# Bidirectional mLSTM recurrence: the decay moved onto the queries, carried and weighted products summed in one PSUM bank, and transposes and value maps cut into 64-row halves

## The chip, the cores and the metric

The kernel runs on one core of one Trainium2 chip. The metric is the device time in microseconds. Three runs of the kernel before gave 1169.3 to 1170.23 us, with a median of 1169.8 us. All data are float32; the big products are float32 values split into a high and a low part.

## The reference

Two blocks follow each other. The change lies in the first, in the recurrence of its mLSTM branch. For each of 4 heads of width 256, for 2 directions and for 8 chunks of 128 positions, it computes

```
b = cumsum(fj);  log_inter = b + m
m_t = max(log_inter, max(log_D))
inter_w = exp(log_inter - m_t)                        # one number per position
s = (q k^T) * exp(log_D - m_t)
num = s v + inter_w * (q C)                           # C is 256 x 256, carried
den = sum(s) + inter_w * (q n)                        # n is carried
h = num / max(|den|, exp(-m_t))
C, n = decay * C + (ws * k)^T v,  decay * n + sum(ws * k)
```

The queries and values are block-diagonal maps, with blocks of 4, of a convolved input and of the input. Both directions are summed, normalised per head, scaled, gated and multiplied by the output weights.

## The kernel before, in words

**Before and after the recurrence.** Input projections by split products (lines 918 to 920, three products for one) run until 487 us, with features on the partitions. The recurrence runs from there to 676 us. Then come the output product of the first block, its normalisation, and the second block.

**The unit.** The recurrence is written out by hand as 64 units: head h, pair p of a head (0 to 7), direction d, so n = 16 h + 2 p + d (`unit`). For a unit, TensorE does in `units` (line 1179): the carried product, queries times state, two matmuls of 257 columns (line 1194), not in the first pair of a head; filler work for the next head; the weighted product, `Pm` times values, one matmul of 257 columns (line 1210); and the state update, weighted keys `kwb` times values, two matmuls (line 1219), not in the last pair. Column 257 is a column of ones, which carries the denominator. The carried product has bank 0 for itself, the weighted one banks 4 to 7 in turn, the update banks 2 and 3, and all filler work bank 1 (`free` is cut to one bank by `del free[1:]`). `take` makes TensorE wait until the last user of a bank has been read out.

**Filler work.** While head h runs, `headwise(h + 1, i)` makes the features of the next head, one i in each of the units 0 to 11 (`FILL`): i from 0 to 3 the queries (line 1135, 512 columns), 4 to 7 the keys turned over (line 1145, four transposes of 128 x 128), 8 to 11 the values (line 1147, four products of 128 x 128 with `bdh`, a 128 x 128 block-diagonal weight). `scores` in units 12 and 14 makes queries times keys (line 1158). `turn_h` turns the normalised output of the head before over (line 1172) at the end of units 7, 9, 11 and 13 (`TURN`). For head 0 the features and scores are made in one piece ahead of the first unit; for head 3 there is no next head, and a few groups of the output product take the filler's place (`AHEAD`).

**ScalarE**, per unit (line 2402): `weight(n + 1)` makes the exponentials `Wb` (line 2368); `spread` issues the DMA that spreads the rows of -m over all partitions four pairs ahead (line 2359); then the carried product is copied out of bank 0, multiplied by `cols[:, 0, r]`, the decay of each position, into `tmpi` or `tmpj` (line 2415); then the filler's banks are copied out (lines 2340 to 2351), outputs of the head before are normalised, split or turned (lines 2399, 2393, 2376).

**GpSimd**, per unit: `Pm` = scores times `Wb` (line 783), `kwb` = keys times a weight per position (line 749), in even units the mask added (line 755), and for the head before the gate and the low half (lines 762 and 770).

**VectorE**, per pair (line 1821): `total` adds `tmp` to the weighted product in its bank (line 1794), `state` updates the state (line 1773, or 1776 in the first pair), then the denominators (lines 1835 to 1837), `output` (lines 1805, 1808), and statistics and skip part (lines 1719, 1725, 1757).

```
                ps = filled(ve, "t_intra", n + 1, "v_h", n + 1)
                if p:
                    ve.wait_ge(s["a_tmp"], upd_of(h, p - 1, d) + 1)
                    ve.tensor_tensor(ps[:, 0:AUG], ps[:, 0:AUG], tmps[p % 2][:, d, :], ALU.add
                                     ).then_inc(s["v_tot"], 1)
```

Here `filled` waits for TensorE's product; the second wait is for ScalarE's scaled copy.

Of the kernel before, what the change touches and what calls it, by code (L numbers as in the profile page):

```python
# [13 lines left out]
P = 128  # L14
# [92 lines left out]
def build(nc, I, out):  # L107
# [64 lines left out]
    nm_t = nc.dram_tensor("nmax", [ROWS, P], F32)  # L172
# [4 lines left out]
    with ctx:  # L177
# [12 lines left out]
        def sem(name):  # L190
# [7 lines left out]
        (u_hi, u_lo, qT0, qT1, kt0, kt1, v0, v1, ST0, ST1, Wb, yt1, tmpj, smzb, h2, Q, y2a, _q, y2b, glu, _h, agb, _b, pTd, pTb) = region(  # L198
# [6 lines left out]
             ("yt1", [P, HALF], F32), ("tmpj", [P, 2, AUG], F32),  # L205
# [23 lines left out]
        def y2(j, part):  # L229

            if j < 4:
# [7 lines left out]
         hc0, yt0, kwb, Amat, hc1, Cst, tmpi, Pm, bdh, gs, nM, cols,  # L239
# [19 lines left out]
             ("tmpi", [P, 2, AUG], F32), ("Pm", [P, 2, P], F32), ("bdh", [P, 2, P], F32),  # L259
# [13 lines left out]
        hcs, tmps = (hc0, hc1), (tmpi, tmpj)  # L273
        gsum = cva[:, 0, :]
        yts = (yt0, yt1)

        def brd(q):
            place = hc1 if q < 4 else wraw
            return place[:, q % 4, :].rearrange("p (d t) -> p d t", d=2)

        def rows_of(q):
            r0, r1 = unit(2 * q)[4], unit(2 * q + 1)[4]
            return bass.AP(nm_t, r0 * P, [[0, P], [(r1 - r0) * P, 2], [1, P]])
# [25 lines left out]
        bank = [ctx.enter_context(nc.psum_tensor(f"bank{i}", [P, 512], F32)) for i in range(4)]  # L309
        wide = [ctx.enter_context(nc.psum_tensor(f"wide{m}", [P, S], F32)) for m in range(2)]  # L310
        bank += [wide[i // 2][:, i % 2 * 512:(i % 2 + 1) * 512] for i in range(4)]
# [14 lines left out]
            "v_tot v_h v_hn v_y1 v_h2 v_lnv v_nmr v_xh v_x2lo v_bnv v_ln2 v_ug v_sp v_yab v_cv2 v_s v_rc "  # L326
            "v_o v_cg v_pT v_y2lo v_r2 v_gain v_out "

            "v_rel a_w0 a_ss a_sd a_uhi a_px a_mixhi a_sz a_yhi a_um a_c a_mz a_gsum a_r a_hq a_st a_W a_tmp a_t1 "
# [20 lines left out]
        FILL = {m: (m,) for m in range(12)}  # L350
# [96 lines left out]
        def _(sp_):  # L447
# [101 lines left out]
            for n in range(16):  # L549
# [19 lines left out]
                if n == 13:  # L569
                    sp_.wait_ge(s["v_r"], 3)  # L570
                    sp_.dma_start(nm_t.ap(), nM[:, :]).then_inc(s["o_rel"], 16)
                    sp_.wait_ge(s["o_rel"], 32)
                    for q in range(4):
                        sp_.dma_start(brd(q), rows_of(q)).then_inc(s[f"l_br{q}"], 16)
# [28 lines left out]
            sp_.wait_ge(s["a_W"], NU)  # L603
            wt(W_OM + 2)
# [74 lines left out]
        def _(g_):  # L679
# [53 lines left out]
            def heads_blocks(h):  # L733

                if h:
                    g_.wait_ge(s["t_hw"], 12 * h)
                else:
                    g_.wait_ge(s["t_gsum"], 2)
# [34 lines left out]
            def units(h):  # L773
                g_.wait_ge(s["a_hq"], 12 * h + 8)
# [117 lines left out]
        def _(pe):  # L892
# [225 lines left out]
            turns, free = [0], [1, 5, 2, 6, 3, 7]  # L1118
# [7 lines left out]
            def headwise(h, i):  # L1126


                n, i = i // 4, i % 4
                if n == 0:  # L1130
# [3 lines left out]
                    ps = fill("a_hq", 12 * h + i + 1)  # L1134
                    mm = pe.matmul(ps[:, :], Amat[:, 2 * h + m, :], cc[:, 2 * h + m, nh * HALF:(nh + 1) * HALF],  # L1135
                                   start=True, stop=True)
                else:
                    ps = fill("a_hq", 12 * h + 4 * n + i + 1)
                    if n == 2 and i == 0:
                        pe.wait_ge(s["g_bdh"], 2 * h + 2)  # L1140
                    for b in range(4):
                        t, m = 2 * i + b // 2, b % 2
                        tt = slice(t * P, (t + 1) * P)
                        if n == 1:
                            mm = pe.transpose(ps[:, b * P:(b + 1) * P], cc[:, 2 * h + m, tt], idn)
                        else:
                            mm = pe.matmul(ps[:, b * P:(b + 1) * P], um[:, 2 * h + m, tt], bdh[:, m, :],  # L1147
                                           start=True, stop=True)
# [1523 lines left out]
```

## Time and profile before

| what | before |
|---|---|
| median of 3 runs (lowest, highest) | 1169.8 us (1169.3, 1170.23) |
| span of the profiled execution | 1168.5 us |
| TensorE matmul busy | 1158.7 us, 99% |
| VectorE busy | 678.5 us, 58% |
| ScalarE busy | 359.2 us, 31% |
| GpSimd busy | 455.9 us, 39% |
| instructions | 17252 |

The span is the time from the first to the last instruction in one profiled execution; no time of its own is given for that execution beside the span, and the median of the runs is 1.3 us above it. Busy shares are averages over stages: TensorE's 99% says that it bounds most of the program, and not what an engine costs inside the recurrence. A matmul's recorded duration includes its way through the array, so the cost of one in a dense row is the distance of the starts, not the mean duration.

### The profile page before, as it was taken

How to read it: one execution, taken by the hardware profiler on the slowest of the kernel's cores; microseconds unless marked ns; L12 is line 12 of the kernel's file. 1: busy time of each engine (PE TensorE's matmuls, PEld its weight loads, DVE VectorE, ACT ScalarE, POOL GpSimd, SP SyncE). 2: the span in 40 equal slices, each digit the busy share in tenths (PEclk: the TensorE clock that was granted, in tenths of full speed). 3: DMA queues.
4: the chain of work that ended last, by engine and by line, in shares of the span. 5: the costliest groups of instructions: out<-in, count | busy, mean ns of one | idle time of the engine just before them, and what ended most of it. 6: DMA issues, size and time to landing. Idle time of an engine off the chain costs nothing.

```text
span 1168.5 us, 17252 instructions
## 1 busy us (share of the span) xinstructions
PE 1158.7 (99%) x6599; PEld 946.1 (81%) x6599; DVE 678.5 (58%) x1249; ACT 359.2 (31%) x720; POOL 455.9 (39%) x437
## 2 busy tenths in 40 slices
PE   9999999999999999999999999999999999999997
PEld 6888888888888868888878888878988887777786
DVE  5645557334368502157777883894699434556668
ACT  6312121100012212445665631242111134553322
POOL 2424222223333223354657656304223323455534
PEclk9999999999999999999999999999999999999999
DMA  7321121343312112300113242123121130133113
GB/s 241 109 81 45 36 81 36 123 152 114 109 36 72 64 64 90 101 23 23 50 34 112 88 171 73 72 100 95 40 88 36 37 100 1 38 122 124 39 38 141
DMA packets 75075, 93.56 MB, mean 80 GB/s; under 512 B 13938, under 2 KB 54090, under 8 KB 74483
## 3 DMA queue, kind: packets, MB, share of 16 engines
q1 hardware_dynamic: 67270, 88.73, 22.7%
q10 hardware_dynamic: 7724, 3.74, 1.2%
q8 instruction: 53, 0.87, 0.3%
q14 instruction: 28, 0.22, 0.1%
HBM read 75.11 MB, written 18.92 MB: 80 GB/s over the span
## 4 chain that ended last, share of the span: by engine, by line
PE 93%; DVE 4%; DMA 1%; ACT 1%; issue 1%; POOL 0%; ACTq 0%; DVEq 0%; POOLq 0%
PE bank L918 22%; PE bank L920 22%; PE bank L919 22%; PE bank L1219 4%; PE bank L1194 4%; PE wide L1210 2%; PE wide L1412 2%; PE bank L1158 1%; PE bank L1147 1%; PE bank L1135 1%; PE wide L920 1%; PE wide L919 1%; PE wide L918 1%; PE bank L1387 1%; DVE h L1910 1%; PE wide L1387 1%
## 5 line engine op out<-in xcount | busy, mean ns | idle before, releaser
L687 POOL CAST whi<-wraw 128x2048 fp32r<-128x2048 f32 x31 | 58.8, 1898 | 454.1 <-PE bank L920 404.1
L918 PE MATMUL bank<-u_hi,wlo 128*128 128x512 f32 x488 | 190.4, 390 | 0.0
L920 PE MATMUL bank<-u_hi,whi 128*128 128x512 f32 x488 | 189.9, 389 | 0.0
L919 PE MATMUL bank<-u_lo,whi 128*128 128x512 f32 x488 | 189.9, 389 | 0.0
L689 POOL TENSOR_TENSOR wlo<-wraw,whi 128x2048 fp32r<-128x2048 f32 x32 | 153.1, 4784 | 3.0 <-ACT whi L2488 0.5
L918 PE MATMUL bank<-x_hi,wlo 128*128 128x512 f32 x312 | 123.5, 396 | 0.0
L920 PE MATMUL bank<-x_hi,whi 128*128 128x512 f32 x312 | 121.6, 390 | 0.0
L919 PE MATMUL bank<-x_lo,whi 128*128 128x512 f32 x312 | 121.5, 389 | 0.0
L918 PEld LDWEIGHTS bank<-u_hi,wlo 128*128 128x128 f32 x488 | 91.6, 188 | 19.9 <-POOL wlo L689 0.8
L920 PEld LDWEIGHTS bank<-u_hi,whi 128*128 128x128 f32 x488 | 91.6, 188 | 19.0
L919 PEld LDWEIGHTS bank<-u_lo,whi 128*128 128x128 f32 x488 | 91.6, 188 | 18.9
L918 PEld LDWEIGHTS bank<-x_hi,wlo 128*128 128x128 f32 x312 | 58.5, 188 | 16.1 <-issue 4.3
L1990 DVE SCALAR_TENSOR_TENSOR wide<-glu,VT,wide 128x1024 f32<-128x1024 f32 x58 | 69.3, 1281 | 0.0
L920 PEld LDWEIGHTS bank<-x_hi,whi 128*128 128x128 f32 x312 | 58.5, 188 | 12.4
L919 PEld LDWEIGHTS bank<-x_lo,whi 128*128 128x128 f32 x312 | 58.6, 188 | 11.7
L862 POOL TENSOR_SCALAR sp<-sp,rcx 128x384 f32<-128x384 f32 (+1 forms) x64 | 37.9, 606 | 76.4 <-DVE rcx L2077 76.4
L1219 PE MATMUL bank<-v,kwb 128*128 128x257 f32 x224 | 58.3, 383 | 0.5 <-DVE Cst L1773 0.3
L1650 DVE SCALAR_TENSOR_TENSOR cva<-um,VT,cva 128x1022 f32<-128x1022 f32 (+1 forms) x32 | 58.0, 1812 | 1.1
L1194 PE MATMUL bank<-Cst,qT 128*128 128x257 f32 x224 | 58.0, 381 | 0.1
L2296 ACT ACTIVATE um<-bank 128x512 f32<-128x512 f32 x16 | 9.6, 599 | 155.7 <-PE bank L920 155.7
L783 POOL TENSOR_TENSOR Pm<-ST,Wb 128x128 f32<-128x128 f32 x64 | 29.1, 455 | 66.0 <-ACT Wb L2368 61.2
L918 PE MATMUL bank<-whi,ym_lo 128*128 128x512 f32 x128 | 51.2, 400 | 0.0
(391 smaller groups left out, 2440.9 us busy)
## 6 DMA issues: line engine op xcount, KB each, us to landing
wraw<-in_w_in SPq DMA_DIRECT2D x26, 1024.0 KB, 5.5
wraw<-in_w_out SPq DMA_DIRECT2D x12, 1024.0 KB, 5.1
xr<-in_x SPq DMA_DIRECT2D x8, 512.0 KB, 7.3
hst<-in_x SPq DMA_DIRECT2D x4, 1024.0 KB, 5.0
hpool<-hst SPq DMA_DIRECT2D x4, 1024.0 KB, 4.1
smz<-mzs SPq DMA_DIRECT2D x16, 256.0 KB, 2.0
h<-hpool SPq DMA_DIRECT2D x4, 1024.0 KB, 7.5
resid<-h SPq DMA_DIRECT2D x8, 512.0 KB, 2.6
```

The costliest lines, as they stand in the source:

```text
L687: g_.tensor_copy(whi[w % 2][:, :, :], wraw[:, :, :]).then_inc(s["w_hi"], 1)
L689: g_.tensor_tensor(wlo[w % 2][:, :, :], wraw[:, :, :], whi[w % 2][:, :, :].bitcast(F32), ALU.subtract).then_inc(s["w_lo"], 1)
L783: g_.tensor_tensor(Pm[:, n % 2, :], STs[h % 2][:, ck, :], Wb[:, n % 2, :], ALU.mult).then_inc(s["g_P"], 1)
L862: g_.tensor_scalar(row, row, rcx[:, x % 2, i:i + 1], 0.5 if g else 1.0, ALU.mult, ALU.mult).then_inc(s["g_nm"], 1)
L918: pe.matmul(ps, al, bh, start=(k == 0), stop=False)
L919: pe.matmul(ps, ah, bl, start=False, stop=False)
L920: return pe.matmul(ps, ah, bh, start=False, stop=(k == nk - 1))
L1194: mm = pe.matmul(ps[:, 0:AUG], q[:, k, ck * P:(ck + 1) * P], Cst[:, d, k, :], start=(k == 0), stop=(k == 1))
L1210: pe.matmul(ps[:, 0:AUG], Pm[:, n % 2, :], v[:, ck, :], start=True, stop=True).then_inc(s["t_intra"], 1)
L1219: mm = pe.matmul(ps[:, 0:AUG], kwb[:, m % 2, k * P:(k + 1) * P], v[:, ck, :], start=True, stop=True)
L1650: ins = ve.scalar_tensor_tensor(acc[:, a0:a1], um[:, j, a0 + sh:a1 + sh], tap(q), acc[:, a0:a1], ALU.mult, ALU.add)
L1990: ins = ve.scalar_tensor_tensor(dst, src, w, acc, ALU.mult, ALU.add)
```

## The change

1. **Decay.** The rows exp(log_inter - m_t), in `r4[:, 0, :]`, are written to DRAM beside the rows of -m, and spread over all partitions with them (256 columns for 128). VectorE multiplies the queries of a chunk by them (`scale_q`, line 1826 of the new code), one pair ahead, into `qsi` or `qsj`. The multiplication by `cols[:, 0, r]` in ScalarE's copy goes, and with it the copy itself.
2. **One bank.** The carried product, of the scaled queries, is written into the bank of the weighted product (`start=(k == 0), stop=False`), and the weighted product is added there by TensorE (`start=(p == 0)`). VectorE's `total` goes. The bank is taken ahead of the carried product.
3. **Halves.** Keys turned over, value maps and, for heads 0 to 2, the output turned over are cut into products of 64 rows and 64 columns: rows 0 to 63 into one bank, rows 64 to 127 into the next. An i now covers 8 blocks of 128 x 128, not 4, and `FILL` puts them into units 4, 6 (keys) and 8, 10 (values). The filler has banks 0 and 1.

The core of the diff:

```diff
-            turns, free = [0], [1, 5, 2, 6, 3, 7]
+            turns, free = [0], [5, 6, 7, 4]
...
+            def both(m, name, value):
+
+                take(2 * m, name, value)
+                return take(2 * m + 1, name, value)
...
+                both(m2, "a_hq", 10 * h + (i + 1 if i < 6 else 2 * i - 4))
+                if i == 6:
+                    pe.wait_ge(s["g_bdh"], 2 * h + 2)
+                for block in range(8):
+                    t, m = i % 2 * 4 + block // 2, block % 2
+                    tt = slice(t * P, (t + 1) * P)
+                    for half in range(2):
+                        rows = slice(64 * half, 64 * half + 64)
+                        out_ = bank[2 * m2 + half][:, block * 64:(block + 1) * 64]
+                        if i < 6:
+                            mm = pe.transpose(out_, cc[rows, 2 * h + m, tt],
+                                              cst[rows, C_ID + 64 * half:C_ID + 64 * half + 64])
                         else:
-                            mm = pe.matmul(ps[:, b * P:(b + 1) * P], um[:, 2 * h + m, tt], bdh[:, m, :],
-                                           start=True, stop=True)
+                            mm = pe.matmul(out_, um[rows, 2 * h + m, tt], bdh[rows, m, rows], start=True, stop=True)
...
-        FILL = {m: (m,) for m in range(12)}
+        FILL = {0: 0, 1: 1, 2: 2, 3: 3, 4: 4, 6: 5, 8: 6, 10: 7}
...
+                    both(0, "a_t1", n + 1)
+                    for b in range(4):
+                        for half in range(2):
+                            rows = slice(64 * half, 64 * half + 64)
+                            mm = pe.transpose(bank[half][:, b * 64:(b + 1) * 64],
+                                              hcs[h % 2][rows, 4 * nh + b, mt * P:(mt + 1) * P],
+                                              cst[rows, C_ID + 64 * half:C_ID + 64 * half + 64])
...
+                    sums = take(4 + n % 4, "v_h", n + 1)
                     if p:
                         i = upd_of(h, p - 1, d)
+                        pe.wait_ge(s["v_qs"], i + 1)
                         pe.wait_ge(s["v_C"], 2 * i + 2)
-                        ps = take(0, "a_tmp", i + 1)
                         for k in range(2):
-                            mm = pe.matmul(ps[:, 0:AUG], q[:, k, ck * P:(ck + 1) * P], Cst[:, d, k, :],
-                                           start=(k == 0), stop=(k == 1))
+                            mm = pe.matmul(sums[:, 0:AUG], scaled_q(i)[:, k, :], Cst[:, d, k, :],
+                                           start=(k == 0), stop=False)
...
-                    ps = take(4 + n % 4, "v_h", n + 1)
-                    pe.matmul(ps[:, 0:AUG], Pm[:, n % 2, :], v[:, ck, :], start=True, stop=True
+                    pe.matmul(sums[:, 0:AUG], Pm[:, n % 2, :], v[:, ck, :], start=(p == 0), stop=True
...
+                    ve.tensor_tensor(scaled_q(i), qTs[h % 2][:, :, ck * P:(ck + 1) * P],
+                                     carried(n // 2, d).unsqueeze(1).to_broadcast([P, 2, P]), ALU.mult
+                                     ).then_inc(s["v_qs"], 1)
...
-                    total(h, n)
+                    if p < NT - 1:
+                        scale_q(h, p + 1)
                     if p or h in (0, NH - 1):
                         state(h, n)
-                    total(h, n + 1)
-                    if p:
-                        ve.wait_ge(s["v_tot"], upd_of(h, p - 1, 1) + 1)
+                    ve.wait_ge(s["t_intra"], n + 2)
...
+                    sp_.wait_ge(s["a_r"], 3)
+                    sp_.dma_start(nm_t.ap()[:, 1, :], r4[:, 0, :]).then_inc(s["o_rel"], 16)
```

**How instructions move, 1.** TensorE, ahead of the first unit, the features of head 0. Before, from the last two query maps to the scores:

```order
L1135 MATMUL bank<-cc,Amat 128x512
L1145 MATMUL wide<-cst,cc 128x128 x4
L1145 MATMUL bank<-cst,cc 128x128 x4
L1145 MATMUL wide<-cst,cc 128x128 x4
L1145 MATMUL bank<-cst,cc 128x128 x4
L1147 MATMUL wide<-bdh,um 128x128 x4
L1147 MATMUL bank<-bdh,um 128x128 x4
L1147 MATMUL wide<-bdh,um 128x128 x4
L1147 MATMUL bank<-bdh,um 128x128 x4
L1158 MATMUL wide<-qT,cc 128x128 x8
```

And now:

```order
L1152 MATMUL wide<-cc,Amat 128x512 x4
L1165 MATMUL bank<-cst,cc 128x64 x32
L1168 MATMUL wide<-bdh,um 128x64 x32
L1178 MATMUL bank<-qT,cc 128x128 x16
L1152 MATMUL bank<-cc,Amat 128x512
```

Sixteen transposes and sixteen value products of 128 columns have become 32 and 32 of 64 columns, in one row behind each other.

**How instructions move, 2.** TensorE, units 4 and 5 of head 0 (`wide` is the pair of banks of the weighted product). Before:

```order
L1194 MATMUL bank<-Cst,qT 128x257 x2
L1145 MATMUL bank<-cst,cc 128x128 x4
L1210 MATMUL wide<-v,Pm 128x257
L1219 MATMUL bank<-v,kwb 128x257 x2
L1194 MATMUL bank<-Cst,qT 128x257 x2
L1145 MATMUL bank<-cst,cc 128x128 x4
L1210 MATMUL wide<-v,Pm 128x257
```

And now:

```order
L1222 MATMUL wide<-Cst,qsj 128x257 x2
L1165 MATMUL bank<-cst,cc 128x64 x16
L1237 MATMUL wide<-v,Pm 128x257
L1246 MATMUL bank<-v,kwb 128x257 x2
L1222 MATMUL wide<-Cst,qsj 128x257 x2
L1237 MATMUL wide<-v,Pm 128x257
```

The 257-column products are as many as before; both units' transposes now stand in one group of 16 halves in unit 4, and unit 5 has no filler.

**How instructions move, 3.** VectorE, one middle pair of head 0. Before:

```order
L1794 TENSOR_TENSOR wide<-wide,tmpj 128x257
L1773 SCALAR_TENSOR_TENSOR Cst<-Cst,cols,bank 128x257 x2
L1794 TENSOR_TENSOR wide<-wide,tmpj 128x257
L1835 TENSOR_TENSOR den<-wide,cols 128x2
L1836 SCALAR_TENSOR_TENSOR den<-wide,den 128x2
L1837 RECIPROCAL den<-den 128x2
```

And now:

```order
L1826 TENSOR_TENSOR qsj<-qT,wraw 128x256 x2
L1800 SCALAR_TENSOR_TENSOR Cst<-Cst,cols,bank 128x257 x2
L1867 TENSOR_TENSOR den<-wide,cols 128x2
L1868 SCALAR_TENSOR_TENSOR den<-wide,den 128x2
L1869 RECIPROCAL den<-den 128x2
```

Two additions in PSUM, one ahead of and one behind the first state update, have become two multiplications with both inputs in SBUF, both ahead of it.

## Rows read from the trace of the kernel before

**Rows 1.** The page: busy time of each engine, share of the span, instructions.

```profile
PE 1158.7 (99%) x6599; PEld 946.1 (81%) x6599; DVE 678.5 (58%) x1249; ACT 359.2 (31%) x720; POOL 455.9 (39%) x437
```

**Rows 2.** Busy by stretch: heads 0, 1, 2, and two pairs late in head 3.

```profile
core 0: us, PE busy (x) PEld busy (x) DVE busy (x) ACT busy (x) POOL busy (x), PEclk, DMA share, GB/s
499.00:542.60 43.60, 43.60 (x234) 37.59 (x234) 27.89 (x82) 19.92 (x45) 19.51 (x41) 1.00 0.09 23
542.60:589.40 46.80, 46.58 (x250) 38.58 (x249) 34.62 (x105) 29.89 (x63) 28.10 (x46) 1.00 0.14 40
589.40:636.30 46.90, 46.68 (x250) 38.36 (x248) 34.82 (x105) 30.30 (x64) 30.49 (x49) 1.00 0.17 46
660.80:671.50 10.70, 10.70 (x53) 8.79 (x52) 9.79 (x27) 6.02 (x14) 10.70 (x15) 1.00 0.18 52
```

**Rows 3.** Timeline of PE: start, time to the last end, what. Head 0's features.

```profile
490.03 0.60 PE L1145 MATMUL wide<-cst,cc 128*128 128x128 f32 x4
...
491.77 1.06 PE L1147 MATMUL wide<-bdh,um 128*128 128x128 f32 x8
...
495.35 1.95 PE L1158 MATMUL wide<-qT,cc 128*128 128x128 f32 x16
```

**Rows 4.** Timeline of PE: transposes in 64-row halves elsewhere, and their neighbours.

```profile
786.23 0.71 PE L1251 MATMUL wide<-cst,h 64*128 64x64 f32 x16
786.87 0.50 PE L1301 MATMUL bank<-x_hi,whi 128*128 128x512 f32 x1
...
937.38 0.39 PE L920 MATMUL bank<-x_hi,whi 128*128 128x512 f32 x1
937.70 1.21 PE L1251 MATMUL wide<-cst,Q 64*128 64x64 f32 x32
938.84 0.50 PE L918 MATMUL bank<-x_hi,wlo 128*128 128x512 f32 x1
939.17 0.39 PE L919 MATMUL bank<-x_lo,whi 128*128 128x512 f32 x1
```

**Rows 5.** Timeline of PE: products (not transposes) on two alternating tiles.

```profile
1063.85 0.88 PE L1412 MATMUL wide<-pT,vt 128*64 128x128 f32 x12
1064.55 0.83 PE L1412 MATMUL wide<-pTc,vt 128*64 128x128 f32 x12
```

**Rows 6.** Timeline of ACT ahead of the first unit: table load, last values, first scores.

```profile
492.80 1.28 ACT L2368 ACT_TABLE_LOAD   x1
...
495.84 0.61 ACT L2345 ACTIVATE v<-bank 128x512 f32<-128x512 f32 x1
497.33 0.60 ACT L2351 ACTIVATE ST<-wide 128x512 f32<-128x512 f32 x1 [0.89 <-PE wide L1158]
```

**Rows 7.** Timeline of PE in head 1: a late unit.

```profile
551.99 1.03 PE L1219 MATMUL bank<-v,kwb 128*128 128x257 f32 x4
553.07 1.11 PE L1194 MATMUL bank<-Cst,qT 128*128 128x257 f32 x4
554.02 0.60 PE L1145 MATMUL bank<-cst,cc 128*128 128x128 f32 x4
```

**Rows 8.** Timeline of ACT and DVE at the same place: the copy and its addition.

```profile
552.47 0.46 ACT L2415 ACTIVATE tmpj<-bank,cols 128x257 f32<-128x257 f32 x1
553.03 0.43 DVE L1794 TENSOR_TENSOR wide<-wide,tmpj 128x257 f32<-128x257 f32 x1 [1.43 <-ACT tmpj L2415]
```

**Rows 9.** Groups of instructions: sum, mean ns, idle before. SBUF-only and PSUM operations of DVE.

```profile
L1794 DVE TENSOR_TENSOR wide<-wide,tmpj 128x257 f32<-128x257 f32 x32 | 13.8, 431 | 18.4 <-PE wide L1210 11.1 <-ACT tmpj L2415 7.1
L1738 DVE TENSOR_SCALAR hc<-hc,mv,rs 128x256 f32<-128x256 f32 x8 | 2.7, 407 | 0.0
```

**Rows 10.** Timelines of DVE and POOL in head 3, at a DVE pass over SBUF alone.

```profile
665.28 0.95 DVE L1757 SCALAR_TENSOR_TENSOR yt<-cc,VT,yt 128x512 f32<-128x512 f32 x1
665.66 0.92 POOL L749 TENSOR_SCALAR kwb<-kt,cols 128x256 f32<-128x256 f32 x1
...
668.22 0.47 POOL L749 TENSOR_SCALAR kwb<-kt,cols 128x256 f32<-128x256 f32 x1
```

More of the change, by code:

```diff
@@ L238, in build @@
          cva, mzs, _m, wgx, gx, gr, ga, wkx, kx, ak,
-         hc0, yt0, kwb, Amat, hc1, Cst, tmpi, Pm, bdh, gs, nM, cols,
+         hc0, yt0, kwb, Amat, hc1, Cst, qsi, Pm, bdh, gs, nM, cols,
          rif, rl, rb, r4, rz, rp, rpc, rms8, rn,
@@ L307, in build @@
         rcx = sb("rcx", [P, 2, 2])
-        bank = [ctx.enter_context(nc.psum_tensor(f"bank{i}", [P, 512], F32)) for i in range(4)]
+        duo = [ctx.enter_context(nc.psum_tensor(f"bank{m}", [P, S], F32)) for m in range(2)]
         wide = [ctx.enter_context(nc.psum_tensor(f"wide{m}", [P, S], F32)) for m in range(2)]
-        bank += [wide[i // 2][:, i % 2 * 512:(i % 2 + 1) * 512] for i in range(4)]
+        duo += wide
+        bank = [duo[i // 2][:, i % 2 * 512:(i % 2 + 1) * 512] for i in range(8)]
         names = (
@@ L1133, in headwise @@
                         pe.wait_ge(s["g_am"], KT)
-                    ps = fill("a_hq", 12 * h + i + 1)
-                    mm = pe.matmul(ps[:, :], Amat[:, 2 * h + m, :], cc[:, 2 * h + m, nh * HALF:(nh + 1) * HALF],
-                                   start=True, stop=True)
[L1137 to L1145, printed above, removed]
-                        else:
-                            mm = pe.matmul(ps[:, b * P:(b + 1) * P], um[:, 2 * h + m, tt], bdh[:, m, :],
-                                           start=True, stop=True)
+                    ps = fill("a_hq", 10 * h + i + 1)
+                    pe.matmul(ps[:, :], Amat[:, 2 * h + m, :], cc[:, 2 * h + m, nh * HALF:(nh + 1) * HALF],
+                              start=True, stop=True).then_inc(s["t_hw"], 1)
+                    return
+                both(m2, "a_hq", 10 * h + (i + 1 if i < 6 else 2 * i - 4))
[10 more added lines that the diff above has]
+                                              cst[rows, C_ID + 64 * half:C_ID + 64 * half + 64])
+                        else:
+                            mm = pe.matmul(out_, um[rows, 2 * h + m, tt], bdh[rows, m, rows], start=True, stop=True)
                 mm.then_inc(s["t_hw"], 1)
             def scores(h, b):
-                pe.wait_ge(s["a_hq"], 12 * h + 4)
+                pe.wait_ge(s["a_hq"], 10 * h + 4)
                 ps = fill("a_st", 2 * h + b + 1)
@@ L1223, in units @@
                         turn_h(h - 1, TURN[n % 16])
-            for i in range(12):
-                headwise(0, i)
+            for i in range(8):
+                headwise(0, i, i % 4)
+            free[:] = [0, 1]
             for b in range(2):
                 scores(0, b)
-            del free[1:]
             for h in range(NH):
@@ L2341, in evac_features @@
                                   ).then_inc(s["a_hq"], 1)
-                elif i < 8:
-                    ac.activation(kts[h % 2][:, t:t + 2, :], pv, ACT.Copy).then_inc(s["a_hq"], 1)
-                else:
-                    ac.activation(vs[h % 2][:, t:t + 2, 0:HD], pv, ACT.Copy).then_inc(s["a_hq"], 1)
+                    return
+                ac.wait_ge(s["t_hw"], 8 * h + i + 1)
+                t = slice(i % 2 * 4, i % 2 * 4 + 4)
+                if i < 6:
+                    ac.activation(kts[h % 2][:, t, :].rearrange("p t (m u c) -> p u (t m) c", m=2, c=64),
+                                  duo[m2][:, :].rearrange("p (u b c) -> p u b c", u=2, c=64), ACT.Copy
+                                  ).then_inc(s["a_hq"], 1)
+                    return
+                for half in range(2):
+                    ac.activation(vs[h % 2][:, t, 0:HD].rearrange("p t (m u c) -> p u t m c", m=2, c=64)[:, half],
+                                  bank[2 * m2 + half][:, :].rearrange("p (t m c) -> p t m c", t=4, c=64), ACT.Copy
+                                  ).then_inc(s["a_hq"], 1)
             def evac_scores(h, b):
@@ L2409, in units @@
                         spread(n // 2 + 4)
[L2410 to L2416 removed]
                     if h + 1 < NH:
[L2418 to L2419 removed]
+                        if m in FILL:
+                            evac_features(h + 1, FILL[m])
                         if m in (12, 14):
```

110 lines of the change are left out of this document (56 added, 54 removed).

## The prediction

> **What bounds the kernel now.** I read the page first, then the busy time by stretch, then single places on the timelines. On the page TensorE is busy 99% of the span and VectorE, the next, 58% [rows 1]. The change touches only the recurrence, from 490 to 676 us, so that is where to look. The busy times by stretch [rows 2] show TensorE busy in 43.60 of 43.60 us while head 0 runs; so what head 0's stretch costs is what TensorE is given. Heads 1 and 2 take 46.80 and 46.90 us. They have four turns of an output more, each of 4 x 0.109 = 0.44 us (the transposes of rows 3: four in 0.43), which makes 43.6 + 1.7 = 45.3; the other 1.5 us per head are waits. Late in head 3, where TensorE has no features to make, GpSimd is busy for all of 10.70 us and VectorE for 9.79: there TensorE is no longer alone at the bound, and a pair takes 5.35 us. TensorE was granted its full clock (1.00, the 2.4 GHz level) in each stretch, so no term is about the clock. The span is 1168.5 us; the runs' median lies 1.3 us above it, outside the recurrence, so I take differences of the span off the median.
>
> **What costs TensorE nothing and gives it nothing.** The decay part leaves TensorE with the same two products of 257 columns per unit, only in another bank. It takes 56 copies from ScalarE and swaps 56 additions on VectorE for 56 multiplications. By itself it can pay only through waits. What pays directly is the halves.
>
> **Step 1, the price of a half.** The trace has transposes in halves elsewhere [rows 4]: 16 of them start at 786.23 and the next matmul at 786.87, 0.64 us; 32 take from 937.70 to 938.84, 1.14 us. So 16 more cost 0.50: 31 ns for one, 62 ns for the two halves of a block, against 0.43 / 4 = 109 ns for a whole transpose [rows 3]; and 0.14 us are fixed. Going in costs more: from 937.38 to 937.70 are 0.32 us, where such a matmul takes 0.23; and the one behind takes 0.33 (938.84 to 939.17), 0.10 too much. That is 0.33 us around each group of halves; behind it here stands a matmul of another kind, whose slow start is 0.08 (553.07 to 554.02 is 0.95, where four take 0.87 [rows 7]). I take 0.31.
>
> A page of the Trainium skill speaks of this: "TensorEngine Tiling (Array Packing)", sections "Theoretical Speedup" and "Key Properties". It gives up to 2 times for 64 rows, and says that changing the tiling mode drains the engine. The rows agree with the drain and put 0.31 us on it; the speed-up they show is 1.75 and not 2. By a full 2 times without the drain all steps on halves together would give about 13 us.
>
> **Step 2, head 0's features.** Keys and values now take from 490.03 to 495.35, 5.32 us [rows 3]. Afterwards there are 16 pairs of key halves and 16 pairs of value halves. A value product is float32 and no transpose, so it goes through twice (eight records for four blocks, 0.89 us). Whether the two halves' passes run side by side, as transposes do, no row shows for this tile form. The nearest are 12 passes of 128 columns on two alternating tiles in 0.70 us, 58 ns each, where whole ones take 111 [rows 5, 3]; so yes. 16 + 32 = 48 slots of 62.5 ns are 3.0, with one change in and out 3.3 us: 2.0 gained. ScalarE takes part of it: its work here is a table load and copies, and its last value copy ends at 496.45 [rows 6]. The amount that it copies stays (the keys' copies are twice as long and half as many), so the first score copy, which began at 497.33, can begin at about 496.6 and end at 497.2. TensorE is back in the first unit at 497.05 and needs that bank at once, so 0.2 to 0.3 us of waiting come. **-1.7 us**, bounds 0 (ScalarE and GpSimd hold it) and -2.0. The second DRAM write ahead of the spread (SyncE's queue, and the stores of the gate's rows behind it) delays the first mask by about 3 us; it is not needed until the first `Wb`, behind the table load at 492.80, so it is covered.
>
> **Step 3, the features of heads 1 to 3.** Keys: 16 x 0.109 = 1.74 us become 2 x (0.50 + 0.31) = 1.62, 0.12 gained. Values: 4 x 0.89 = 3.57 become 2 x (1.00 + 0.31) = 2.62, 0.95 gained. Three heads of 1.07: **-3.2 us**. Bounds: 0.25 us around a group gives -3.9, 0.40 gives -2.1.
>
> **Step 4, the turned outputs.** Four blocks in halves cost 0.25 + 0.31 = 0.56 us against 0.44: a loss of 0.12 each, since the group is too short for its changes. Eight in heads 1 and 2: **+1.0 us**. Four more in head 3 lie beside work that is the bound there.
>
> **Step 5, waits that go.** In heads 1 and 2 ScalarE is late after its table loads. Its copy out of bank 0 runs from 552.47 to 552.93, and TensorE starts the next carried product at 553.07 instead of 552.86, then needs 0.08 to come up to speed [rows 7, 8]. The addition on VectorE is late by the same copy (idle 1.43 us, ended by it [rows 8]), and the update behind it waits too. That is 2 x 0.29 us per head, on waits that no longer exist: **-1.15 us**, bounds 0 and -1.5 (the waits between a turn and the next filler, on ScalarE's other copies, stay). Next in line are `Wb`, `Pm` and `kwb`, which come earlier as ScalarE has 56 x 0.47 us less.
>
> **Step 6, the scaled queries.** One addition on VectorE takes 0.43 us with PSUM, a pass of 256 columns in SBUF 0.41 [rows 9]: the same. They are made a pair ahead, so TensorE waits for the state and not for them. But they read two inputs in SBUF. Late in head 3 the one such pass of VectorE (665.28) goes along with a `kwb` of 0.92 us on GpSimd, which takes 0.47 when it is alone, and takes 0.95 itself [rows 10]. So the two engines shut each other out, and now two passes per pair do so. The additions, with an input in PSUM, did not. In head 3 GpSimd has no idle time [rows 2]: two passes of 0.35 to 0.4 us more in each of two to three pairs are +1.4 to +2.4 us; VectorE's idle time for ScalarE, some 0.5 us per pair, goes. **+1.5 us**, bounds -0.5 and +2.5. In heads 0 to 2 GpSimd is busy 20 to 30 of 44 to 47 us and hides it.
>
> The page "SBUF — State Buffer" of the Trainium skill, section "SBUF: two separate sides", has this as a rule: a VectorE operation with two SBUF inputs and a GpSimd operation that reads SBUF lock each other out for the whole instruction. The trace agrees, 0.92 against 0.47 us.
>
> **Sum.** -1.7 - 3.2 + 1.0 - 1.15 + 1.5 = -3.6. From 1169.8 this gives **1166.2 us**; what lies behind the recurrence moves with it, since the output product and all behind it wait for TensorE.
>
> **Rivals.**
> - *The lock costs in heads 1 and 2 as well.* From unit 9 on GpSimd has the gate of the head before, and a pair of it is 5.35 us in all heads; two locks make it 6.1, against TensorE's 5.7 to 7. A late `Pm` or `kwb` costs at least 0.29 us [rows 7]. Once in each of the last four pairs of two heads: +2.3, so 1168.5, no difference that counts. For it: GpSimd's full row in head 3. Against it: 16 to 19 us of idle time per head [rows 2].
> - *Nothing is gained ahead of unit 0 and at the waits* (ScalarE decides both): 1169.0.
> - *The passes of the value halves don't overlap*, so that it ends slower. The two passes of one half use the same rows of the array; if the other half's issue waits behind the second, a slot holds one pass and not two. A group of 8 blocks is then 32 x 0.0625 + 0.31 = 2.3 us instead of 1.31, and 1.79 before. Eight groups: +8 on the forecast, 1174.2. It decides from about 0.19 us per block on, where the sum is zero. Against it: rows 5.
>
> **How the numbers follow.** A measurement of this kernel tells 0.2%, 2.3 us, from no change. Forecast, with steps between their bounds: 0.70, nearly all of it below 1167.5. Lock everywhere or nothing gained at the start: 0.20. Slower: 0.10, most of it the passes, some of it waits on the new order that I don't see. The lower end is the good bound of each step together with a head 3 that loses nothing (-2.0 - 3.5 + 1.0 - 1.3 - 0.3 = -6.1, 1163.7); the upper end takes in the second rival, 1169.2.
>
> **What would show it.** Right: 4 blocks of value halves in some 0.5 us and a group behind a switch of 0.3; features of head 0 in 3.3 us; heads 0 to 2 at about 42.5, 45.2 and 45.2 us; no wait on ScalarE's copy of the carried product; head 3 longer by about 1.5 us with `kwb` or the scaling often at twice its time. Wrong: value halves at 0.25 us per block; waits of TensorE on `Pm`, `kwb` or the scaled queries in heads 0 to 2; or a head 3 that is shorter.

## The result and the profile after

The changed kernel takes 1172.97 us (median of 8 runs, 1172.6 to 1174.44) against 1169.54 for the kernel before (8 runs beside it, 1169.3 to 1170.23): ratio 1.0029, 95% interval 1.0019 to 1.0039. It is 3.4 us slower, where 3.6 us less were forecast. The profiled execution took 1172.75 us with a span of 1170.9 us, in front of 1168.5 before.

The busy row of its page answers to [rows 1]: TensorE 240 instructions more, ScalarE 64 copies fewer.

```profile
PE 1159.4 (99%) x6839; PEld 942.0 (80%) x6839; DVE 685.2 (59%) x1249; ACT 333.6 (28%) x656; POOL 463.6 (40%) x437
```

The stretches of [rows 2] were not cut at the same events in each head; head 2 ended 2.1 us too early there. I cut both traces anew, from the first weighted product (`Pm`) of a head to that of the next, and in head 3 to that of its last unit. In the changed kernel all cuts lie at the second pass of that product, 0.22 us behind the first, which leaves the lengths as they are. Busy time by stretch, the kernel before:

```profile
499.80:543.36 43.56, 43.56 (x234) 37.55 (x233) 28.06 (x83) 19.66 (x45) 19.48 (x40) 1.00 0.10 24
543.36:590.21 46.85, 46.63 (x250) 38.63 (x249) 34.94 (x107) 29.94 (x62) 28.15 (x47) 1.00 0.14 40
590.21:638.45 48.24, 48.02 (x257) 39.77 (x256) 35.92 (x110) 30.43 (x63) 31.83 (x50) 1.00 0.19 51
638.45:676.73 38.28, 37.89 (x178) 31.35 (x177) 33.45 (x101) 21.76 (x46) 27.10 (x42) 1.00 0.36 119
```

and the same of the changed kernel:

```profile
498.91:543.09 44.18, 44.18 (x282) 36.99 (x281) 27.26 (x85) 12.40 (x29) 19.68 (x40) 1.00 0.15 48
543.09:590.85 47.76, 47.02 (x314) 37.56 (x313) 35.75 (x106) 23.54 (x46) 30.88 (x47) 1.00 0.20 62
590.85:639.86 49.01, 48.54 (x321) 38.77 (x320) 37.55 (x111) 24.06 (x47) 34.22 (x50) 1.00 0.23 71
639.86:679.80 39.94, 38.24 (x194) 30.93 (x193) 36.22 (x99) 18.50 (x37) 29.43 (x43) 1.00 0.37 128
```

So the heads take 0.62, 0.91, 0.77 and 1.66 us more, 3.96 in all; the stretch from head 0's first query map to its first weighted product takes 0.41 less (12.77 against 13.18, from the starts in the trace). Together +3.55, close to the 3.4 of the medians. Head 0 has no idle time of TensorE, so it has more to do; in heads 1, 2 and 3 TensorE's idle time grows, from 0.22, 0.22 and 0.39 us to 0.74, 0.47 and 1.70.

The spans differ by 2.4 us and not by 3.55, because two other parts are shorter in the changed kernel's trace. The part ahead of the first query map takes 0.7 us less, and over all traces of kernels with the change it varies by 0.6. The part behind the recurrence takes 0.47 less, and in all twelve traces of the changed kernel and its variants it takes 0.4 to 0.55 less than in the one trace before. Most of it is one wait that only the trace before has: there the weights of a later product (`wraw`) arrive late, VectorE waits 0.42 us for ScalarE's copy of them, and TensorE starts 0.4 us late behind VectorE (timeline of PE, before):

```profile
785.21 1.09 PE L1273 MATMUL wide<-cst,h 128*128 128x128 f32 x8 [0.24 <-DVE h L1910]
```

So the sums below, which count head 0's features and the heads alone, are up to 0.5 us higher than what the medians show.

**Halves.** Timeline of PE in head 0's features, which answers to [rows 3], and at a group of values in head 0's units:

```profile
489.44 1.21 PE L1165 MATMUL bank<-cst,cc 64*128 64x64 f32 x32
490.49 3.73 PE L1168 MATMUL wide<-bdh,um 64*128 64x64 f32 x64
494.15 3.84 PE L1178 MATMUL bank<-qT,cc 128*128 128x128 f32 x32
...
518.55 1.03 PE L1222 MATMUL wide<-Cst,qsj 128*128 128x257 f32 x4
519.51 2.00 PE L1168 MATMUL bank<-bdh,um 64*128 64x64 f32 x32
521.45 0.70 PE L1237 MATMUL wide<-v,Pm 128*128 128x257 f32 x2
521.98 0.60 PE L1246 MATMUL bank<-v,kwb 128*128 128x257 f32 x2
```

The 16 keys take 1.05 us (489.44 to 490.49), 66 ns a block, where 62 were forecast and a whole one takes 109. The 16 values take 3.66 us (to 494.15), 229 ns a block, and whole ones took 0.89 / 4 = 223 [rows 3]. Halves give nothing there: 0.09 of the 3.66 us is the change back to whole tiles, and the rest is 223 ns a block again. In the group at 519.51 eight blocks take 1.94 us, and the switch is paid on both sides: 0.96 from 518.55 where such a product takes 0.87, and 0.53 behind where 0.43 is usual.

**Waits.** Timeline of PE at head 1's first carried products, then of DVE at the same place:

```profile
545.02 0.60 PE L1237 MATMUL wide<-v,Pm 128*128 128x257 f32 x2
545.45 1.03 PE L1246 MATMUL bank<-v,kwb 128*128 128x257 f32 x4
547.23 1.11 PE L1222 MATMUL wide<-Cst,qsj 128*128 128x257 f32 x4 [0.74 <-issue]
```

```profile
544.78 0.76 DVE L1803 COPY Cst<-bank 128x257 f32<-128x257 f32 x2 [1.11 <-PE bank L1246]
545.46 0.39 DVE L1752 BATCH_NORM_AGGREGATE mv<-bn 128x2 f32<-128x6 f32 x2
545.76 0.72 DVE L1746 BATCH_NORM_STATS2 bn<-hc 128x6 f32<-128x256 f32 x2
546.40 1.07 DVE L1826 TENSOR_TENSOR qsj<-qT,wraw 128x256 f32<-128x256 f32 x2
```

The state has been there since about 545.5, but the product that uses it also needs the scaled queries. VectorE makes these (L1826) behind the state's copy and the statistics of head 0's last outputs; the first of the two passes ends at 547.13, and TensorE starts at 547.23. "issue" on PE's row is that wait: 1.78 us from the product before, where 0.87 is usual, 0.91 lost. In head 2, ahead of the product at 594.76, 0.6 us are lost in the same way. The lock has a share in both: the first pass takes 0.73 us in head 1 and 0.85 in head 2, beside GpSimd's work, where one takes 0.41 alone.

The third place is head 3. Timelines of DVE and of POOL there:

```profile
652.63 1.44 DVE L1826 TENSOR_TENSOR qsj<-qT,wraw 128x256 f32<-128x256 f32 x2
653.99 0.86 DVE L1800 SCALAR_TENSOR_TENSOR Cst<-Cst,cols,bank 128x257 f32<-128x257 f32 x2
```

```profile
652.89 0.89 POOL L768 TENSOR_TENSOR wraw<-wraw,msk 128x256 f32<-128x256 f32 x1
653.80 0.58 POOL L796 TENSOR_TENSOR Pm<-ST,Wb 128x128 f32<-128x128 f32 x1
```

Two scaling passes need 1.44 us beside GpSimd's work, where two take 0.83 otherwise; the state's update stands behind them, and TensorE behind that. Waits of PE in the recurrence:

```profile
PE bank L1246 <- DVE Cst L1800: 1.7, 3, 1.0
PE wide L1222 <- issue: 1.2, 2, 0.7
```

(us in total, times, longest). The copy of [rows 7, 8] is gone, and no wait on it is left.

### The profile page after: what moved, and what is told of

Same layout as the page of the kernel before. It is cut to its first block, busy times and chain, and to the rows that moved or that the text cites. A ratio compares the mean times of both kernels' runs of the same rounds, so it can differ in the third digit from the quotient of the medians.

```text
span 1170.9 us, 17563 instructions
## 1 busy us (share of the span) xinstructions
PE 1159.4 (99%) x6839; PEld 942.0 (80%) x6839; DVE 685.2 (59%) x1249; ACT 333.6 (28%) x656; POOL 463.6 (40%) x437
## 4 chain that ended last, share of the span: by engine, by line
PE 97%; DVE 2%; DMA 0%; issue 0%; ACT 0%; ACTq 0%; DVEq 0%
PE bank L931 24%; PE bank L933 23%; PE bank L932 23%; PE wide L1222 4%; PE bank L1246 4%; PE wide L1237 2%; PE wide L1439 2%; PE bank L1178 1%; PE bank L1168 1%; PE wide L931 1%; PE wide L933 1%; PE wide L932 1%; PE bank L1152 1%; PE bank L1414 1%; PE wide L1414 1%; PE bank L1426 1%
## 5 line engine op out<-in xcount | busy, mean ns | idle before, releaser
L796 POOL TENSOR_TENSOR Pm<-ST,Wb 128x128 f32<-128x128 f32 x64 | 33.7, 526 | 66.4 <-ACT Wb L2408 60.2
L1800 DVE SCALAR_TENSOR_TENSOR Cst<-Cst,cols,bank 128x257 f32<-128x257 f32 x96 | 41.8, 477 | 21.2 <-PE bank L1246 21.0
```

Of the source, the lines that this page charges most:

```text
L796: g_.tensor_tensor(Pm[:, n % 2, :], STs[h % 2][:, ck, :], Wb[:, n % 2, :], ALU.mult).then_inc(s["g_P"], 1)
L1800: ins = ve.scalar_tensor_tensor(Cst[:, d, k, :], Cst[:, d, k, :], cols[:, 4, r:r + 1], pu[:, 0:AUG], ALU.mult, ALU.add)
```

## The experiments

Theory: the value halves don't pay (their passes don't shorten), and the scaled queries sit in VectorE's order where TensorE has to wait for them, at the start of a head and, stretched by GpSimd, in head 3. Rival: what costs is the order of evacuation and the halves' copies, or the turned outputs. What no run varies is the new grouping of the filler work, 8 blocks at a time over two banks: every run below has it. "Head times" below are those from weighted product to weighted product as above. A ratio is against the kernel before on the same chip.

**One part undone or alone.** e1: the value maps as whole blocks (the copies out of the bank likewise).

```
-  mm = pe.matmul(out_, um[rows, 2 * h + m, tt], bdh[rows, m, rows], start=True, stop=True)
+  if half == 0:
+      whole = bank[2 * m2 + block // 4][:, block % 4 * P:(block % 4 + 1) * P]
+      mm = pe.matmul(whole, um[:, 2 * h + m, tt], bdh[:, m, :], start=True, stop=True)
```

> The changed kernel, with only its value maps made of whole 128 x 128 products again (still 8 blocks per filler, two banks). Theory A (a pass of a value product costs 0.11 us however few columns it has, so that halves only add the switch): the six groups in heads 0 to 2 lose 0.35 us each and head 0's features 0.1, so 2.2 us faster than the changed kernel, about 1170.8 us; a group of 8 blocks back at 1.79 us. Theory B (the loss comes from the scaled queries and waits): within 0.5 us of the changed kernel, 1173.

Measured: 1171.34 us (1170.64 to 1171.71), 1.0011 [1.0002, 1.0020]. Heads 0 to 2 take 43.49, 47.12 and 48.48 us, 0.69, 0.64 and 0.53 less than with halves; head 3 and the part ahead of head 0 are unchanged. The 16 value blocks ahead of unit 0 cost the same whole or in halves (12.77 us from the first query map either way), where they share one switch with the keys. Two groups a head cost 0.31 each on average, which is the price of one switch from the prediction.

e2: the turned outputs whole again.

```
-  for half in range(2):
-      rows = slice(64 * half, 64 * half + 64)
-      mm = pe.transpose(bank[half][:, b * 64:(b + 1) * 64],
-                        hcs[h % 2][rows, 4 * nh + b, mt * P:(mt + 1) * P],
-                        cst[rows, C_ID + 64 * half:C_ID + 64 * half + 64])
+  mm = pe.transpose(bank[0][:, b * P:(b + 1) * P],
+                    hcs[h % 2][:, 4 * nh + b, mt * P:(mt + 1) * P], idn)
```

> The changed kernel, with only the turned outputs of heads 0 to 2 whole again. Theory A: the eight turns in heads 1 and 2 cost 0.58 us in halves and 0.44 whole, so 1.2 us faster, about 1171.8; the four in head 3 lie beside VectorE's and GpSimd's bound and give 0 to 0.6 more. Theory B: no change, 1173.

Measured: 1172.85 us, 1.0023 [1.0014, 1.0032]. Heads: 44.18, 47.62, 49.16, 39.84; 0.09 us less in all, where 1.2 were expected. Behind a turn TensorE waits for the scores' bank: from the end of the update ahead of the turn to the scores are 1.53 us with a whole turn (577.69 to 579.22 in head 1) and 1.49 with halves, so there the halves' cost lies in a wait. In head 2 something else hides it: with whole turns the wait for the scaled queries at its start is 1.04 us and not 0.59. Without that growth the halves of heads 1 and 2 would cost 0.4 us, an estimate from these rows.

e3: the keys whole again.

```
-  mm = pe.transpose(out_, cc[rows, 2 * h + m, tt],
-                    cst[rows, C_ID + 64 * half:C_ID + 64 * half + 64])
+  if half == 0:
+      whole = bank[2 * m2 + block // 4][:, block % 4 * P:(block % 4 + 1) * P]
+      mm = pe.transpose(whole, cc[:, 2 * h + m, tt], idn)
```

> The changed kernel, with only the keys' transposes whole again. Theory A: head 0's features lose 0.7 us, the six groups in the heads change by under 0.04 each: 1173.6, slower than the changed kernel by 0.6. Theory B: no change.

Measured: 1174.0 us, 1.0035 [1.0021, 1.0048]. The part ahead of head 0 takes 0.75 us more (13.52), the heads 0.07, 0.07, 0.08 and 0.24 more. Keys in halves gain 1.2 us by this, of which the 0.24 in head 3, where no keys are made, have no cause that I can show.

e4: the decay part alone; keys, values and turns are all whole (e1, e2 and e3 together).

> The changed kernel with values, keys and turns all whole: what is left of the change is the decay on the queries and the shared bank. Theory A: 2.2 + 1.2 - 0.7 = 2.7 us faster than the changed kernel, 1170.3, so about 0.7 us slower than the kernel before, with the waits on the scaled queries at the start of heads 1 and 2 and in head 3 still there. Theory B (the decay is the whole loss): 1173, with the waits making 3.4 us against the kernel before.

Measured: 1171.92 us (1171.41 to 1173.47), 1.0016 [1.0007, 1.0024]. Heads: 43.56, 47.35, 48.70, 39.83, which is 0, +0.50, +0.46 and +1.55 on the kernel before. So 2.5 us of the 3.55 are the decay part (with the new grouping of the filler, which this run keeps), and the halves the other 1.0, where I had expected 2.7 for the halves.

**The order of the scaled queries.** e5, on e1: the queries of a head's first carried pair are scaled in the last pair of the head before, ahead of the statistics.

```
-  if p < NT - 1:
+  if p and p < NT - 1 or n == 0:
       scale_q(h, p + 1)
+  if p == NT - 1 and h < NH - 1:
+      scale_q(h + 1, 1)
```

> e1 (values whole), with the queries of a head's first carried pair scaled one pair earlier, ahead of the statistics of the head before. Theory C (TensorE waits at the start of heads 1 and 2 for scaled queries that stand on VectorE behind the statistics): the waits of 0.98 and 0.68 us go, 1.6 us faster than e1, about 1169.7. Theory D (VectorE is simply behind by its doubled passes, and the wait moves to the next thing it makes): under 0.5 us.

Measured: 1169.1 us (1168.77 to 1171.64), 0.9998 [0.9989, 1.0006]. Heads 1 and 2 fall from 47.12 and 48.48 to 46.12 and 47.53; head 3 keeps its 39.96. The wait at head 1's start is gone (timeline of PE of e5):

```profile
544.59 0.60 PE L1239 MATMUL wide<-v,Pm 128*128 128x257 f32 x2
545.02 1.03 PE L1248 MATMUL bank<-v,kwb 128*128 128x257 f32 x4
545.89 1.03 PE L1224 MATMUL wide<-Cst,qsj 128*128 128x257 f32 x4
```

e7, on e5: the state's update ahead of the scaling in each pair.

```
+  if p or h in (0, NH - 1):
+      state(h, n)
   if p and p < NT - 1 or n == 0:
       scale_q(h, p + 1)
   if p == NT - 1 and h < NH - 1:
       scale_q(h + 1, 1)
-  if p or h in (0, NH - 1):
-      state(h, n)
```

> e5 with, in every pair, the first state update ahead of the scaling. Theory O: TensorE's waits of 1.2, 0.58 and 0.65 us in head 3, for the state's banks, fall by what the two passes take there (1.4 us each), 1.5 us or more faster than e5, about 1168. Theory L (the lock's cost is throughput of VectorE and GpSimd and only moves): under 0.4 us faster than e5.

Measured: 1169.15 us, 0.9993 [0.9984, 1.0002]. Head 3 gains 0.40 (39.56), head 2 loses 0.54 (48.07). The order moves the wait and gains nothing in sum. It also brings the passes beside other work of GpSimd: 31 of the 56 take over 0.5 us, where 16 did in e5, and in head 2 TensorE waits 0.34 us for a late `Pm` (591.10).

**The lock.** e6, on e1: the scaling reads one tensor, with a column as a scalar; the decay at each position is left out, so that only one factor per partition is applied.

```
-  ve.tensor_tensor(scaled_q(i), qTs[h % 2][:, :, ck * P:(ck + 1) * P],
-                   carried(n // 2, d).unsqueeze(1).to_broadcast([P, 2, P]), ALU.mult
+  ve.tensor_scalar(scaled_q(i), qTs[h % 2][:, :, ck * P:(ck + 1) * P],
+                   cols[:, 0, r:r + 1], 1.0, ALU.mult, ALU.mult
```

> e1 with the scaling as a pass with one SBUF input and a number per partition, of the same size and at the same place; the decay of each position is left out, so the numbers are not the recurrence's. Theory L (the passes and GpSimd shut each other out because the passes read two SBUF inputs): two passes take 0.75 us and not 1.07 to 1.45, kwb stays at 0.48, and the waits fall by at least half: 1.5 to 2 us faster than e1, 1169.5. Theory O (the order is the cause: two passes stand ahead of the state update and behind the statistics, locked or not): the waits shrink only by the passes' own shortening, 0.6 us or less in all, 1170.8.

Measured: 1169.64 us (1169.55 to 1170.42), 1.0000 [0.9991, 1.0009]. Head 3 takes 39.02, 0.95 less than in e1, but the test isn't clean: the passes are shorter when alone, and still stretched. One line's instructions of e6 (ns: least/median/most):

```profile
L1828 DVE TENSOR_SCALAR qsi<-qT,cols x28: 331/355/2610, 490.5 to 665.6; 128x256 f32<-128x256 f32 x28
L1828 DVE TENSOR_SCALAR qsj<-qT,cols x28: 334/541/1351, 503.8 to 671.0; 128x256 f32<-128x256 f32 x28
```

The longest there (579.87, 1.35 us) begins under GpSimd's gate (L775) and ends 0.15 us behind it, so it waits for that too. So I needed a pass of equal length whose second input is in PSUM. Data for it are there only once the denominators have been read, so the pair e9 and e10 has the scaling there. e9, on e5: the two `if` blocks of e5 stand behind the denominators.

> e5 with the two scaling passes of each pair behind the denominators and ahead of the outputs, so that they no longer stand ahead of the first state update. Theory L (a lock costs VectorE and GpSimd time that no order gives back): head 3 up to its last weighted product stays within 0.5 us of e5's 39.96, the run within 0.5 us of 1169.1. Theory O (order): head 3 at 38.5 or less, 1167.7.

Measured: 1180.01 us (1179.85 to 1180.17), 1.0087 [1.0074, 1.0101], over 10 us above either expectation: both had looked at head 3, and heads 0 to 2 take 4.2, 2.9 and 3.3 us more than in e5. e10, on e9: the second input is the bank with the sums, and the operation a comparison instead of a product; the decay of the carried product is left out.

```
-  carried(n // 2, d).unsqueeze(1).to_broadcast([P, 2, P]), ALU.mult
+  wide[(at_q[0]) % 2][:, 0:2 * P].rearrange("p (k c) -> p k c", k=2), ALU.is_ge
```

> e9 with the second input of each scaling pass taken from the weighted product's PSUM bank and not from the spread rows in SBUF, and a comparison in place of the product; the decay is left out, so the numbers are not the recurrence's. Same size, same place, same number of passes. Theory L: no pass over 0.5 us, kwb back at 0.48 us but for the pass of the skip part, head 3 shorter than e9's by 1 to 1.7 us and the run at about 1168. Theory O: the same times as e9 within 0.4 us.

Measured: 1173.66 us (1173.26 to 1174.39), 1.0033 [1.0021, 1.0045], 6.35 us less than e9. The scaling's line in e9 and then in e10:

```profile
L1828 DVE TENSOR_TENSOR qsj<-qT,wraw x26: 411/496/1493, 520.6 to 684.0; 128x256 f32<-128x256 f32 x26
L1828 DVE TENSOR_TENSOR qsi<-qT,wraw x24: 410/496/1483, 527.2 to 678.2; 128x256 f32<-128x256 f32 x24
```

```profile
L1830 DVE TENSOR_TENSOR qsi<-qT,wide x28: 412/417/422, 502.4 to 672.1; 128x256 f32<-128x256 f32 x28
L1830 DVE TENSOR_TENSOR qsj<-qT,wide x28: 411/418/422, 509.0 to 677.3; 128x256 f32<-128x256 f32 x28
```

and GpSimd's weighted keys, groups of instructions of e9 and then of e10:

```profile
L762 POOL TENSOR_SCALAR kwb<-kt,cols 128x256 f32<-128x256 f32 x56 | 32.5, 581 | 2.6 <-PE bank L1248 2.5
```

```profile
L762 POOL TENSOR_SCALAR kwb<-kt,cols 128x256 f32<-128x256 f32 x56 | 29.3, 523 | 2.5 <-PE bank L1248 2.4
```

With an input in PSUM no scaling pass is stretched; with both in SBUF the median is 496 and the longest 1493 ns. Five of GpSimd's weighted keys still take 0.91 to 1.02 us in e10, each beside VectorE's pass of the skip part (L1786), which has its inputs in SBUF. Head 3 takes 38.69 against 40.59, 1.90 less. The run stays above the 1168 us expected, since e9's late order is still in it: TensorE waits 3.6 us in all ahead of carried products. e9 also shows what a late scaling costs in every pair: waits of PE in its recurrence,

```profile
PE wide L1224 <- issue: 8.2, 19, 0.9
PE bank L1248 <- DVE Cst L1805: 0.6, 2, 0.4
```

**What a value pass is made of.** e8, on e1: each whole value block gets 64 moving columns for 128, so half of each value block is left out.

```
-  mm = pe.matmul(whole, um[:, 2 * h + m, tt], bdh[:, m, :], start=True, stop=True)
+  mm = pe.matmul(whole, um[:, 2 * h + m, tt], bdh[:, m, 0:64], start=True, stop=True)
```

> e1 (whole value products, 128 rows, 128 stationary columns) with 64 moving columns for 128; half of each value block is left out. If a pass lasts as long as its stationary side takes to load, the starts stay 0.11 us apart; if it lasts as long as its moving columns, they are 0.055 apart and a group of 8 blocks takes 0.9 us for 1.79.

Measured: 1171.18 us (one run). Timeline of PE in e8:

```profile
519.68 1.89 PE L1170 MATMUL bank<-bdh,um 128*128 128x64 f32 x16
521.41 0.65 PE L1239 MATMUL wide<-v,Pm 128*128 128x257 f32 x2
```

and in e1:

```profile
519.23 1.95 PE L1170 MATMUL bank<-bdh,um 128*128 128x128 f32 x16
521.01 0.60 PE L1239 MATMUL wide<-v,Pm 128*128 128x257 f32 x2
```

16 passes take 1.73 us with 64 columns and 1.78 with 128. The first start to the second is 0.055 us with 64 columns, and all that follow are 0.111 or 0.112 apart, as with 128. Halving what moves through doesn't shorten a value pass.

**A better version.** e11, on e5: both directions of a pair are scaled in one pass of 512 columns.

```
-  for n in (16 * h + 2 * p, 16 * h + 2 * p + 1):
...
-      ve.tensor_tensor(scaled_q(i), qTs[h % 2][:, :, ck * P:(ck + 1) * P],
-                       carried(n // 2, d).unsqueeze(1).to_broadcast([P, 2, P]), ALU.mult
...
+  q0 = qTs[h % 2][:, :, p * P:(p + 1) * P]
+  qs = bass.AP(q0.tensor, q0.offset, [list(q0.ap[0]), [(NT - 1 - 2 * p) * P, 2], [S, 2], [1, P]])
+  rows = spread_rows(n // 2)[:, :, P:2 * P].unsqueeze(2).to_broadcast([P, 2, 2, P])
+  ve.tensor_tensor((qsi, qsj)[i // 2 % 2][:, :, :, :], qs, rows, ALU.mult).then_inc(s["v_qs"], 2)
```

> e5 with one scaling pass of 512 columns per pair for both directions, for two of 256: 28 passes, about 0.69 us each if alone, and one chance per pair of being shut out by GpSimd instead of two. Theory L: head 3 up to its last weighted product takes 39.2 to 39.6 us instead of 39.96, and the run comes to 1168.5 with the bound below the kernel before's. Theory O: no change from e5, 1169.1.

Measured: 1168.51 us (1168.05 to 1169.2), 0.9987 [0.9978, 0.9996]. Most of its passes (L1829):

```profile
L1829 DVE TENSOR_TENSOR qsj<-qT,wraw x13: 675/691/946, 515.0 to 669.4; 128x512 f32<-128x512 f32 x13
L1829 DVE TENSOR_TENSOR qsi<-qT,wraw x12: 675/691/943, 520.2 to 663.6; 128x512 f32<-128x512 f32 x12
```

0.69 us for what two passes did in 0.83, and 0.95 at most beside GpSimd where two took up to 1.44. Head 3 takes 39.32 us, 0.64 less than in e5. This version has the decay on the queries, keys and turns in halves and whole values. It is the fastest of all, by 1.5 us on the kernel before beside it (1170.04): its interval ends below 1, though the gain is less than the 0.2% that I called a difference.

## Why the prediction was wrong

**Step 1, the price of a half: right for transposes, wrong for value products.** The keys took 66 ns a block (62 forecast). The step's failure is the use of that slot for values in steps 2 and 3.

**Steps 2 and 3, "Whether the two halves' passes run side by side ... so yes".** This is the step that failed most. They do run side by side: by the starts in the trace the passes of both halves begin 7 ns apart (520.009 and 520.016), so the third rival's mechanism, a slot that holds one pass, is wrong too. But the next pair follows at 520.121, 0.112 us later, and not 0.062. A pair of half passes takes as long as one whole pass, so nothing is gained and each group's switches (0.31) are added: e1 gets 0.62 back per head. It was 229 ns a block at the start and 1.94 / 8 = 243 within a group, beyond the rival's point of decision at 0.19. That rival's consequence, slower, came, and its 0.25 us per block is near too: the values cost +1.8 us by e1, where steps 2 and 3 had about -1.3 and -2.85, so 6 us on the forecast, where the rival had 8. [Rows 5] misled: their 58 ns belong to tiles 64 columns wide, while the value tiles load 128; the row gives no price for a tile with 64 rows and 128 columns, and I took "runs side by side" and "takes half" for one thing. e8 excludes the moving columns as the cause. What is left differs in the weight loads, from groups of PEld in the changed kernel (mean ns behind the sum):

```profile
L1168 PEld LDWEIGHTS wide<-bdh,um 64*128 64x128 f32 x64 | 3.7, 188 | 0.0
L1165 PEld LDWEIGHTS bank<-cst,cc 64*128 64x128 f32 x32 | 1.1, 139 | 0.8 <-issue 0.8
```

Same tile, same shape, 188 ns for a product and 139 for a transpose. That the load sets the slot fits these two and e8. But the recorded load alone doesn't tell the slot: in the kernel before, whole transposes record 141 ns and hold 109, not 62. No run varied the load, so what sets a product's slot stays open.

A rule of the Trainium skill that I weighed there ("TensorEngine Tiling (Array Packing)", section "Theoretical Speedup") gives up to 2 times for 64 rows. The trace agrees for keys, 1.66 times, and shows no gain for values, 0.97 times.

Of step 2's -1.7 us only -0.4 came: keys -0.7 as forecast, values nothing by themselves, and the switch +0.3 (0.1 ahead of the keys, 0.1 behind the values, 0.1 in the first score). The wait for ScalarE's score copy, 0.2 to 0.3 in the forecast, didn't come: the scores follow each other without a gap behind the first. Of step 3 the keys' -0.12 a head is -0.07 (e3).

**Step 4, turns: the size was wrong.** +1.0 forecast, +0.1 measured (e2), and some 0.4 by the estimate that leaves out the longer wait at head 2's start in e2. TensorE waited for the scores' bank behind a turn before, and waits less now. I had costed busy time where there was in part cover.

**Step 5, waits that go: right in size.** They are gone. In e5, where nothing stands in their place, heads 1 and 2 are 0.73 and 0.71 us shorter than before, 1.44 in all, of which keys are 0.14 (e3), so 1.3 or more with the turns' cost. In e4 they are 0.96 longer with 1.95 of new waits in them, which leaves 1.0. Forecast were 1.15. That the gain is the missing copy's, and not that of the filler's new grouping over two banks, no run separates.

**Step 6, the scaled queries: right in size for head 3, wrong on where else.** Head 3 got 1.55 us longer with the decay part alone (e4), +1.5 forecast, and e9 against e10 shows the lock to be the cause of 1.9 there, in the late order. This mechanism is the rule of the page "SBUF — State Buffer" of the Trainium skill, section "SBUF: two separate sides", that the prediction cited; the runs agree: the longest pass is 1493 ns in e9 and 422 in e10. But "They are made a pair ahead, so TensorE waits for the state and not for them" doesn't hold in the first pair of heads 1 and 2. There VectorE comes to that pair's work only behind the copy of the head's first state, which itself waits for the head's first update, and behind statistics that were harmless before. By e5 that is 1.00 and 0.95 us, 2.0 in all, some of it the lock on the first pass. This unlisted wait took the place of step 5's gain. I had read VectorE's order for a steady pair and not for the seam between heads. The first rival (the lock in heads 1 and 2, "once in each of the last four pairs") didn't happen in those pairs: with the seams mended, TensorE is busy for all of 46.12 and 47.51 us of heads 1 and 2 in e11, which has the same scaling in longer passes. What did come of it is the lock's share at the seams, and one late `Pm` in e7.

**The sum.** Forecast -3.6, measured +3.55 by the traces. The decay part: the seams +2.0, head 3 +1.55 and step 5's gain of 1.0 to 1.3 make +2.2 to +2.5, and e4 has +2.5, where steps 5 and 6 had +0.35. The halves: values +1.8 (e1), keys -1.2 (e3), turns +0.1 (e2) are +0.7; undone together they are worth 1.04 (the changed kernel against e4). The 0.3 between are a switch that keys and values share ahead of head 0: with the keys whole, values in halves take 13.52 us there (e3) and whole ones 13.19 (e4), while with the keys in halves both take 12.77. Steps 2 to 4 had -3.9. So of the 7.2 us between forecast and measurement some 6.0 are the values and 2.0 the seams, less 0.9 for the turns and 0.4 for the keys. The range missed since it had no case between "side by side and half as long" and "one after the other", and the latter was given less than a tenth. Its lower end doesn't add up from the bounds that the steps name, either: -2.0 - 3.9 + 1.0 - 1.5 - 0.5 is -6.9, and the sum there has -3.5, -1.3 and -0.3 for three of them.

## What to carry to other kernels

Split a product into row halves only after a row shows that this very tile (rows, columns, kind of operation) has shorter slots; running side by side is not the same as taking half, and every group pays for its switches. When an operation is put into an in-order engine's queue "a pair ahead", follow that queue over the seams between outer loops, where the pair ahead doesn't exist. A VectorE pass with both inputs in SBUF can cost the length of GpSimd's instruction on top where both engines are full, so merge such passes, or keep an input in PSUM.

## What the runs showed of the hardware that I had not expected

Two half products on separate rows start 1 to 7 ns apart and still hold a slot of 0.112 us, while two half transposes on the same tiles hold 0.062 us. Product passes with 64 moving columns start 0.111 us apart, as those with 128 do (e8, e1), but for the first of a group, 0.055. A VectorE pass with one tensor input in SBUF and a column as scalar was stretched as well, from 0.34 to 1.35 us (e6), while GpSimd was at work, which the two-input reading of the lock doesn't cover; no run isolated it.
